# One inference step of a hybrid S5/HGRN2 decoder: HGRN's first level with 32 weight columns, sample values spread by transfers, state-space table products in four partition groups

## Chip, core and metric

The kernel runs on one core of a Trainium2 chip. The core has five engines with a queue each: PE (TensorE), DVE (VectorE), ACT (ScalarE), POOL (GpSimd) and SP (SyncE, which here only issues transfers). They meet through semaphores. The metric is the device time of one execution, in microseconds (us), as the median of several runs.

## What is computed

A two-layer trunk over 512 prompt tokens and 8 sample tokens, 1024 wide, in f32. Each layer adds half an FFN, a mixer, a cross-attention and half an FFN. The mixer is S5 in layer 0 and HGRN2 (8 heads, 128x128 state) in layer 1. Cut to what the change touches:

```python
# S5: 64 groups of 16 channels, each with a 64-dim complex diagonal state
bu = jnp.einsum('btgc,gpc->btgp', ug, b_bar)
a_cum, x_cum = lax.associative_scan(combine, (a_seq, bu), axis=1)
h = x_cum + a_cum * h0[:, None]
y = jnp.einsum('btgp,gcp->btgc', h, c).real + d * ug

# HGRN2 per token (the prompt is done in chunks of 64 tokens; a sample is one step from its given state)
# S_t = diag(f_t) S_{t-1} + k_t v_t^T ,  o_t = S_t^T q_t
att = jnp.einsum('bthk,bshk,btshk->bhts', qc, kc, decay)     # decay: product of f between s and t, causal
s_new = jnp.exp(btot)[..., None] * s + jnp.einsum('bshk,bshv->bhkv', k_dec, vc)
```

## The kernel before

**Linear layers.** All activations lie transposed (channels on partitions, 520 token columns). Weights stream from HBM tile by tile: SP loads `raw` (L965), ACT rounds it to `w_hi` (L1329), DVE makes the rest `w_lo` (L1826), and PE multiplies `w_hi` by both parts of the activations (L3017) and `w_lo` by the upper part (L3022). SP loads slot `j` of a pair again as soon as DVE has made the low part of what lay in it (`lo_ready`). Each engine runs its instructions in the order in which they are written; small work for the mixers is written between the chunks of the linear layers.

**State-space tables (155 to 320 us).** During layer 0's first FFN, POOL builds tables in eight rounds (`table_part`, L736 to L738): `sFe` for the inputs, then `sGe` for the outputs, and counts `s5_tables` after each. PE turns `sFe` (groups F, L2559) and forms the products K of `sGe` with `bZ` (L2565), to which it adds a diagonal `dD` (L2568). A group K has four pairs `u`; for each, two products of 32 rows and 128 columns and one of 16 columns are added up in `bank[0:32, u * 128:...]`. ACT copies the bank to `sKst` (L1466), from which SP writes a block matrix to HBM (L945). Groups 0 to 3 stand in `ffn1_out0`, groups 4 to 7 in `ffn1_in1`.

**HGRN (1540 to 1815 us).** `hg_in` handles one head per turn, spread over three turns: turn `h` projects head `h` (four chunks of weights: forget gate, queries, values, gate), works on head `g = h - 1` and finishes head `e = h - 2`. PE's groups are numbered in one list, `made`, and group `q` uses PSUM bank `q % 4`; it waits until the bank's last group has been emptied. For head `g`: V and K (transposes, L2798), A (attention within chunks by levels: level 32, 16 and 8 pair the later half of a block with its earlier half, L2810; then the rest, L2813), D (increments of the state, L2836), B (L2818: the value vector of each sample, broadcast to all partitions by transposing a column with step 0), O (outputs, L2851 and L2859). For head `e`: S (the samples' outputs, L2784), T, N and R. A level-32 product of a 64-token chunk takes all 64 tokens of `lvl` as weights and the 32 later ones as moving columns; DVE then copies only the wanted part under a mask (`causal`, L2183).

DVE makes the values (`hgV`, L2187), the states (`hS`, L2201 and L2205), then the samples' states `sS` from group B's banks (L2315), then the next low weights. SP stores `hS` and `sS` (L908, L910) and loads the samples' old states (L921).

**The end of HGRN.** When the last head is done, `hg_out` begins: its first two chunks are multiplied head by head (`projected`, L2896), between the last heads' groups.

## Time and profile before

| | |
|---|---|
| median of 3 runs | 2366.99 us (2365.1 to 2368.97) |
| the profiled execution | 2364.88 us |
| its span | 2363.1 us |
| PE, DVE, ACT, POOL busy | 99%, 55%, 37%, 26% |

An instruction's row gives its start, its duration and how many were merged. Matmuls overlap, so what one costs is the distance from its start to the next one's. PE records an f32 product as two matmuls and an f32 transpose as one. The idle time in brackets names what the engine waited for.

### The profile page before, as it was taken

What the parts mean: (1) busy time and instruction counts of PE and PEld (TensorE: products, weight loads), DVE (VectorE), ACT (ScalarE), POOL (GpSimd) and SP (SyncE); (2) the same over time, 40 slices, a digit from 0 to 9 for tenths busy, and PEclk for the clock granted to TensorE, in tenths of its full rate; (3) what the DMA queues carried; (4) which work ended last, traced back from release to release, by engine and by line L of the source; (5) the groups of instructions that cost most, each with busy time, mean ns of one, the idle gap of its engine ahead of it and who ended that gap; (6) DMA issues with size and microseconds to landing.
All of it is one profiled execution on the core that took longest, in us unless ns stands there. A gap on an engine that the chain in (4) does not pass through costs nothing.

```text
span 2363.1 us, 50146 instructions
## 1 busy us (share of the span) xinstructions
PE 2341.2 (99%) x21043; PEld 2280.2 (96%) x21043; DVE 1292.9 (55%) x1906; ACT 871.4 (37%) x1399; POOL 608.2 (26%) x591
## 2 busy tenths in 40 slices
PE   8999999999999999999999999999999999999999
PEld 8999999889979999999999999999999979999999
DVE  6653643864576543445543344577778666443443
ACT  4422333543233231232333233267775233321323
POOL 4779958331103000004121010432222102000003
PEclk9999999999999999999999999999999999999999
DMA  6456445563463333333543333333332653333332
GB/s 169 128 156 151 119 123 156 182 184 107 148 242 101 95 91 91 98 104 87 169 119 106 105 104 116 86 99 103 109 104 81 214 188 90 98 94 94 98 93 95
DMA packets 483707, 289.19 MB, mean 122 GB/s; under 512 B 22289, under 2 KB 466962, under 8 KB 482514
## 3 DMA queue, kind: packets, MB, share of 16 engines
q1 hardware_dynamic: 477856, 280.66, 40.3%
q0 software_dynamic: 560, 1.84, 0.6%
q10 hardware_dynamic: 5122, 4.25, 0.5%
q8 instruction: 129, 2.11, 0.4%
q14 instruction: 40, 0.33, 0.0%
HBM read 258.86 MB, written 27.85 MB: 121 GB/s over the span
## 4 chain that ended last, share of the span: by engine, by line
PE 89%; DVE 4%; POOL 3%; ACT 2%; DMA 1%; issue 1%; SPq 0%; DVEq 0%; POOLq 0%; ACTq 0%
PE lin L3017 50%; PE lin L3022 25%; PE mis L2511 3%; POOL sTmp L737 1%; PE mis L2648 1%; PE mis L2631 1%; POOL sGe L738 1%; PE lin L2598 1%; POOL sGe L736 1%; PE lin L2979 1%; POOL sFe L738 1%; PE lin L2648 0%; DMA raw<-in_xattn_w_kv_dram 0%; PE lin L2760 0%; DVE w_lo L1826 0%
## 5 line engine op out<-in xcount | busy, mean ns | idle before, releaser
L1826 DVE TENSOR_TENSOR w_lo<-raw,w_hi 128x1024 fp32r<-128x1024 f32 (+1 forms) x322 | 463.4, 1439 | 297.7 <-ACT w_hi L1329 297.1
L1329 ACT ACTIVATE w_hi<-raw 128x1024 fp32r<-128x1024 f32 (+1 forms) x328 | 364.9, 1113 | 305.7 <-PE lin L3022 251.3
L3017 PE MATMUL lin<-a_rear,w_hi 128*128 128x264 f32 x3552 | 455.5, 279 | 0.0
L3017 PE MATMUL lin<-a_front,w_hi 128*128 128x256 f32 x3552 | 451.5, 279 | 1.1 <-DVE a_rear L1839 0.7
L3017 PEld LDWEIGHTS lin<-a_rear,w_hi 128*128 128x128 f32 x3552 | 432.6, 188 | 0.0
L3017 PEld LDWEIGHTS lin<-a_front,w_hi 128*128 128x128 f32 x3552 | 424.4, 188 | 4.6 <-issue 1.9
L3022 PE MATMUL lin<-a_rear,w_lo 128*128 128x264 f32 x1776 | 245.2, 278 | 0.0
L3022 PE MATMUL lin<-a_front,w_lo 128*128 128x256 f32 x1776 | 240.5, 277 | 0.9 <-DVE w_lo L1826 0.9
L2390 DVE SCALAR_TENSOR_TENSOR xT<-lin,xT 128x520 f32<-128x520 f32 (+1 forms) x87 | 60.8, 699 | 322.2 <-PE lin L3022 321.5
L1062 POOL TENSOR_TENSOR acc<-xT 128x520 f32<-128x520 f32 x8 | 12.2, 1520 | 864.0 <-DVE xT L2390 835.9
L3022 PEld LDWEIGHTS lin<-a_rear,w_lo 128*128 128x128 f32 x1776 | 223.8, 188 | 0.0
L3022 PEld LDWEIGHTS lin<-a_front,w_lo 128*128 128x128 f32 x1776 | 219.5, 188 | 1.6 <-DVE w_lo L1826 1.5
L1740 ACT ACTIVATE f_front<-t 128x256 fp32r<-128x256 f32 (+1 forms) x88 | 36.9, 419 | 395.1 <-DVE t L2371 395.1
L3017 PE MATMUL lin<-f_rear,w_hi 128*128 128x264 f32 x1386 | 178.1, 281 | 0.0
L3017 PEld LDWEIGHTS lin<-f_rear,w_hi 128*128 128x128 f32 x1386 | 170.5, 188 | 0.1
L3017 PE MATMUL lin<-f_front,w_hi 128*128 128x256 f32 x1386 | 170.3, 276 | 0.0
L3017 PEld LDWEIGHTS lin<-f_front,w_hi 128*128 128x128 f32 x1386 | 163.3, 188 | 0.1
L1736 ACT ACTIVATE t<-t 128x520 f32<-128x520 f32 x88 | 56.5, 642 | 278.6 <-DVE t L2365 278.6
L2369 DVE TENSOR_TENSOR t<-lin,rstd 128x520 f32<-128x520 f32 x88 | 61.5, 699 | 158.5 <-PE lin L3022 158.4
L1066 POOL TENSOR_TENSOR sqt<-xT 128x520 f32 (+1 forms) x54 | 81.9, 1517 | 211.0 <-DVE xT L2390 148.9
L3017 PE MATMUL lin<-g_all,w_hi 128*128 128x264 f32 (+1 forms) x1024 | 128.8, 278 | 0.0
L3017 PEld LDWEIGHTS lin<-g_all,w_hi 128*128 128x128 f32 x1024 | 122.8, 188 | 1.1 <-DVE g_all L1966 1.1
(512 smaller groups left out, 3207.9 us busy)
## 6 DMA issues: line engine op xcount, KB each, us to landing
raw<-in_ffn_w_in_dram SPq DMA_DIRECT2D x176, 512.0 KB, 3.9
raw<-in_ffn_w_out_dram SPq DMA_DIRECT2D x64, 704.0 KB, 4.6
kc<-in_cache_mem_k_dram SPq DMA_DIRECT2D x32, 512.0 KB, 7.0
vc<-in_cache_mem_v_dram SPq DMA_DIRECT2D x16, 1024.0 KB, 9.4
raw<-in_hg_w_in_dram SPq DMA_DIRECT2D x32, 512.0 KB, 4.3
raw<-in_xattn_w_kv_dram SPq DMA_DIRECT2D x16, 512.0 KB, 4.4
raw<-in_s_w_glu_dram SPq DMA_DIRECT2D x16, 512.0 KB, 4.1
raw<-in_xattn_w_q_dram SPq DMA_DIRECT2D x16, 512.0 KB, 3.9
```

The source lines that it names most:

```text
L736: link(eng.tensor_tensor(out[:, e], pv[0], mv[e], ALU.mult))
L738: link(eng.tensor_tensor(out[:, e], out[:, e], tmp, sign))
L1066: step.link(pool.tensor_tensor(sqt[:], tile(xT, m), tile(xT, m), ALU.mult))
L1329: act.activation(w_hi[:, j, 0:kt, :], raw[:, j, 0:kt, :], ACT.Copy).then_inc(hi_ready, 1)
L1736: act.activation(t2[:], t1[:], ACT.Silu).then_inc(gate_out, 1)
L1740: ins = act.activation(tile(out, i), t3[:, cols], ACT.Copy)
L1826: dve.tensor_tensor(low_weights(n, j), raw[:, j, 0:kt, :], w_hi[:, j, 0:kt, :].bitcast(F32), ALU.subtract).then_inc(lo_ready, 1)
L2369: step.link(dve.tensor_tensor(t4[:], lflat(1), rstd[:], ALU.mult))
L2390: dve.scalar_tensor_tensor(out=tile(xT, m), in0=lflat(j), scalar=scale, in1=tile(xT, m), op0=ALU.mult, op1=ALU.add)\
L2511: ins = pe.matmul(kv_bank(c)[:, 0:NM], w[:, e, k, :], x[:, k, :], start=k == 0 and u == 0, stop=k == KD - 1 and u == 2)
L3017: pe.matmul(lpart(j, half), high[:, k, :], (x_lo if u else x_hi)[half][:, k, :], start=start and u == 0 and k == 0, stop=False)
L3022: ins = pe.matmul(lpart(j, half), low[:, k, :], x_hi[half][:, k, :], start=False, stop=k == kt - 1)
```

## The change

1. **Table products.** The four pairs `u` of a group K write to `bank[32 * u:32 * u + 32, 0:128]` rather than to four column ranges of partitions 0 to 31. The eight long products are issued with `u` in the inner loop, and then the four short ones. `sKst` is 128x128 rather than 32x512.
2. **Samples' values.** The groups B are gone. SP stores the eight value columns of a head to a scratch tensor `hg_v` in HBM (`values_out`) and loads that tensor's 4 KB to each of 128 partitions (`vB`, `values_spread`); DVE reads `vB`. The semaphore `sampled` takes the place of B's emptied banks, and `values` on DVE waits until the store before the last has read `hgV`.
3. **Level 32.** The weights are the first 32 tokens of the chunk, and the result goes to 32 partitions of the 64. The other 32 are under the mask.

```diff
@@ -310,6 +310,9 @@
     sRow = at("sRow", [P, 2, P], F32, o_tmp + TILE)
+
+    vB = [at(f"vB{e}", [P, NS, P], F32, (o_hid + 6 * HTILE, o_tmp + 5 * TILE)[e]) for e in range(2)]
+    hg_v = nc.dram_tensor("hg_v", (HH, NS, P), F32, kind="Internal").ap()
     rT = at("rT", [P, NT // 4], F32, o_tmp + 4 * TILE)
@@ -326,7 +329,7 @@
     sGe = [at(f"sGe{e}", [P, 2, 4, CS + 1, SC], F32, o_s0 + 4608 * e) for e in range(2)]
-    sKst = at("sKst", [2 * SC, 4, P], F32, o_s0 + 31360)
+    sKst = at("sKst", [P, P], F32, o_s0 + 31360)
     dD = at("dD", [P, KD, SC], F32, o_s0 + 11520)
@@ -451,7 +454,8 @@
            "scaled_dve", "front", "state_out", "s_decay", "s_out", "squares", "inverse")}
-    rows_in = [sem(f"rows_in{b}") for b in range(NS)]
+    rows_in = [sem(f"rows_in{b}") for b in range(4)]
+    spread_out, spread_in, sampled = sem("spread_out"), sem("spread_in"), sem("sampled")
     consts_done = sem("consts_done")
@@ -624,7 +628,7 @@
         if 0 <= g < HH:
-            made += [("D", (g, 0), "dve"), ("D", (g, 1), "dve"), ("B", (g, 0), "dve"), ("B", (g, 1), "dve")]
+            made += [("D", (g, 0), "dve"), ("D", (g, 1), "dve")]
             made += [("O", (g, 0), "act"), ("O", (g, 1), "act")]
@@ -906,8 +910,23 @@
                 sp.dma_start(o_["hg_p"][0, 0, h], hS[:, NHC - 1, :]).then_inc(hg["state_out"], 16)
-                HG.emptied_of(sp, "B", (h, 1))
+                sp.wait_ge(sampled, h + 1)
                 sp.dma_start(o_["hg_s"][0, :, h].rearrange("b k v -> k b v"), sS[h % 2][:]).then_inc(hg["s_out"], 16)
+
+            def values_out(h):
+
+                sp.wait_ge(used[0], first_pair["hg_in", 1] + 2 * h + 2)
+                sp.dma_start(hg_v[h].rearrange("b v -> v b"), hgV[h % 2][:, SEQ:NT],
+                             allow_slow_non_contiguous=True).then_inc(spread_out, 16)
+
+            def values_spread(h):
+
+                sp.wait_ge(spread_out, 16 * (h + 1))
+                if h >= 2:
+                    sp.wait_ge(sampled, h - 1)
+                    sp.wait_ge(spread_in, 16 * h)
+                src = bass.AP(tensor=hg_v.tensor, offset=h * NS * P, ap=[[0, P], [P, NS], [1, P]])
+                sp.dma_start(vB[h % 2][:], src).then_inc(spread_in, 16)
 
@@ -942,7 +961,8 @@
                                           ap=[[row, SC], [SC * row - SC, CS], [1, P]])
-                            sp.dma_start(dst, sKst[SC * g:SC * (g + 1), u:u + 1, :].to_broadcast([SC, CS, P]))\
+                            r0 = 2 * SC * u + SC * g
+                            sp.dma_start(dst, sKst[r0:r0 + SC, :].unsqueeze(1).to_broadcast([SC, CS, P]))\
                                 .then_inc(s5_k_out, 16)
@@ -968,6 +988,8 @@
                             s5_matrices(i)
+                        if first and j == 0 and ST[n][0] == "hg_out":
+                            values_spread(HH - 1)
                         if first and j == 0 and ST[n][0] == "xo":
@@ -990,8 +1012,13 @@
                             sample_states_in(i // 2)
-                        elif i >= 4:
-                            states(i // 2 - 2)
+                            if i >= 3:
+                                values_spread(i // 2 - 1)
+                        elif i >= 2:
+                            values_out(i // 2 - 1)
+                            if i >= 4:
+                                states(i // 2 - 2)
+                    values_out(HH - 1)
                     return
@@ -1463,7 +1490,7 @@
                         wait(act, s5_k_out, 16 * CS * a)
-                        act.activation(sKst[:], bank[0:2 * SC, :].rearrange("p (j n) -> p j n", j=4), ACT.Copy)\
+                        act.activation(sKst[:], bank[:, 0:P], ACT.Copy)\
                             .then_inc(s5p_void["act"], 1)
@@ -1644,7 +1671,7 @@
                         if h >= 2:
-                            G.emptied_of(act, "B", (h - 2, 1))
+                            act.wait_ge(sampled, h - 1)
                             act.wait_ge(hg["scaled_pool"], POOLS * (h - 1))
@@ -2184,6 +2211,8 @@
                     dve.wait_ge(chunk_done, 2 * p + 3)
+                    if p >= p0 + 4:
+                        dve.wait_ge(spread_out, 16 * ((p - p0) // 2 - 1))
                     dve.tensor_tensor(hgV[b][:], lflat(0), rstd[:], ALU.mult).then_inc(used[0], 1)
@@ -2306,17 +2335,16 @@
                     if 0 <= g < HH:
+                        dve.wait_ge(spread_in, 16 * (g + 1))
                         for f in range(2):
-                            q = G.at("B", (g, f))
                             dve.wait_ge(hg["s_decay"], 2 * g + f + 1)
-                            dve.wait_ge(hg["fill"], q + 1)
                             for u in range(4):
...
                                 ins = dve.scalar_tensor_tensor(
-                                    out=sS[g % 2][:, s_], in0=hg_bank(q)[:, u * P:(u + 1) * P],
+                                    out=sS[g % 2][:, s_], in0=vB[g % 2][:, s_],
                                     scalar=hgK[g % 2][:, SEQ + s_:SEQ + s_ + 1], in1=sS[g % 2][:, s_],
                                     op0=ALU.mult, op1=ALU.add)
-                            ins.then_inc(hg["void_dve"], 1)
+                        ins.then_inc(sampled, 1)
                     if h == HH:
@@ -2560,13 +2588,14 @@
                         pe.wait_ge(s5_tables, 2 * a + 2)
+                        rows = [slice(2 * SC * u, 2 * SC * (u + 1)) for u in range(4)]
+                        for e in range(2):
+                            for u in range(4):
+                                pe.matmul(bank[rows[u], 0:P], bZ[:, e, 4 * a + u, :, :].rearrange("p g c -> p (g c)"),
+                                          sGe[a % 2][:, e, u, 0:CS, :], start=e == 0, stop=False, skip_group_check=True)
                         for u in range(4):
-                            for e in range(2):
-                                pe.matmul(bank[0:2 * SC, u * P:(u + 1) * P],
-                                          bZ[:, e, 4 * a + u, :, :].rearrange("p g c -> p (g c)"),
-                                          sGe[a % 2][:, e, u, 0:CS, :], start=e == 0, stop=False)
-                            ins = pe.matmul(bank[0:2 * SC, u * P:u * P + SC], ident[:, 2 * SC * u:2 * SC * (u + 1)],
-                                            dD[:, a, :], start=False, stop=True)
+                            ins = pe.matmul(bank[rows[u], 0:SC], ident[:, rows[u]], dD[:, a, :], start=False, stop=True,
+                                            skip_group_check=True)
                     ins.then_inc(s5p_fill, 1)
@@ -2778,7 +2807,7 @@
                 if what == "S":
-                    G.emptied_of(pe, "B", (a, 1))
+                    pe.wait_ge(sampled, a + 1)
                     for b in range(NS):
@@ -2807,15 +2836,12 @@
                             late = lvl[u][:, c].rearrange("p (b a t) -> p b a t", a=2, t=level)[:, :, 1, :]
-                            ins = pe.matmul(bank[rows, t * HC // 2:(t + 1) * HC // 2].rearrange("p (b t) -> p b t", t=level),
-                                            lvl[u][:, c], late, start=True, stop=True)
+                            early = level if 2 * level == HC else HC
+                            ins = pe.matmul(bank[rows.start:rows.start + early, t * HC // 2:(t + 1) * HC // 2]
+                                            .rearrange("p (b t) -> p b t", t=level),
+                                            lvl[u][:, c.start:c.start + early], late, start=True, stop=True)
                         else:
                             ins = pe.matmul(bank[rows, t * HC:(t + 1) * HC], dgK[:, c], dgQ[:, c], start=True, stop=True)
-                elif what == "B":
-                    h, f = a
-                    for u in range(4):
-                        b = SEQ + 4 * f + u
-                        ins = pe.transpose(bank[:, u * P:(u + 1) * P], hgV[h % 2][:, b:b + 1].to_broadcast([P, P]), ident[:])
                 else:
@@ -2934,8 +2960,6 @@
                         hg_increments(g)
-                        hg_group("B", (g, 0))
-                        hg_group("B", (g, 1))
                     if h == HH:
```

PE at a group K. Before (the transposes of `sTF`, then the group, then the next chunk):

```order
L2559 MATMUL mis<-ident,sTF_235 128x128 x3
L2565 MATMUL mis<-sGe_199,bZ 32x128 [waits s5_tables,s5p_void_dve]
L2565 MATMUL mis<-sGe_199,bZ 32x128
L2568 MATMUL mis<-dD,ident 32x16
L2565 MATMUL mis<-sGe_199,bZ 32x128 x2
L2568 MATMUL mis<-dD,ident 32x16
L2565 MATMUL mis<-sGe_199,bZ 32x128 x2
L2568 MATMUL mis<-dD,ident 32x16
L2565 MATMUL mis<-sGe_199,bZ 32x128 x2
L2568 MATMUL mis<-dD,ident 32x16
L3017 MATMUL lin<-f_rear_61,w_hi 128x264 [waits used0,hi_ready]
```

And after:

```order
L2587 MATMUL mis<-ident,sTF_237 128x128 x3
L2594 MATMUL mis<-sGe_201,bZ 32x128 [waits s5_tables,s5p_void_dve]
L2594 MATMUL mis<-sGe_201,bZ 32x128 x7
L2597 MATMUL mis<-dD,ident 32x16 x4
L3041 MATMUL lin<-f_rear_61,w_hi 128x264 [waits used0,hi_ready]
```

The products and the waits are the same; the short ones have moved behind the long ones.

SP at the end of HGRN, from the last loads of `hg_w_in` to the stores of the last head. Before:

```order
L965 DMA raw<-in_hg_w_in_dram 128x8x128 [waits lo_ready] x2
L921 DMA sS_177<-in_state_hgrn_dram 128x8x128 [waits hg_fill,hg_s_out]
L965 DMA raw<-in_hg_w_out_dram 128x8x128 [waits lo_ready] x2
L908 DMA out_hg_p_dram<-hS 128x128 [waits hg_void_dve]
L910 DMA out_hg_s_dram<-sS_176 128x8x128 [waits hg_void_dve]
L908 DMA out_hg_p_dram<-hS 128x128 [waits hg_void_dve]
L910 DMA out_hg_s_dram<-sS_177 128x8x128 [waits hg_void_dve]
```

And after (`hg_v<-hgV` is `values_out`, `vB<-hg_v` is `values_spread`; the three in the middle belong to the heads 6, 7 and 7):

```order
L985 DMA raw<-in_hg_w_in_dram 128x8x128 [waits lo_ready] x2
L940 DMA sS_177<-in_state_hgrn_dram 128x8x128 [waits hg_fill,hg_s_out]
L929 DMA vB_187<-hg_v 128x1024 [waits spread_in,sampled,spread_out]
L919 DMA hg_v<-hgV_163 128x8x1 [waits used0]
L985 DMA raw<-in_hg_w_out_dram 128x8x128 [waits lo_ready]
L929 DMA vB_188<-hg_v 128x1024 [waits spread_in,sampled,spread_out]
L985 DMA raw<-in_hg_w_out_dram 128x8x128 [waits lo_ready]
L912 DMA out_hg_p_dram<-hS 128x128 [waits hg_void_dve]
L914 DMA out_hg_s_dram<-sS_176 128x8x128 [waits sampled]
L912 DMA out_hg_p_dram<-hS 128x128 [waits hg_void_dve]
L914 DMA out_hg_s_dram<-sS_177 128x8x128 [waits sampled]
```

The first load of `hg_w_out` now stands behind the store of head 7's values, which waits for `used0`, and the second behind the load of `vB`, which waits for that store.

## Rows read from the trace of the kernel before

**Rows 1.** The page: engine busy time (us, share, instructions), and the chain's shares.

```profile
PE 2341.2 (99%) x21043; PEld 2280.2 (96%) x21043; DVE 1292.9 (55%) x1906; ACT 871.4 (37%) x1399; POOL 608.2 (26%) x591
...
PE 89%; DVE 4%; POOL 3%; ACT 2%; DMA 1%; issue 1%; SPq 0%; DVEq 0%; POOLq 0%; ACTq 0%
```

**Rows 2.** Timeline of PE, first group K: start, us, engine, line, operation, out<-in, count.

```profile
157.70 0.62 PE L2565 MATMUL mis<-sGe,bZ 128*32 128x128 f32 x4
158.16 0.21 PE L2568 MATMUL mis<-dD,ident 128*32 128x16 f32 x2
158.22 0.60 PE L2565 MATMUL mis<-sGe,bZ 128*32 128x128 f32 x4
...
159.80 2.39 PE L3017 MATMUL lin<-f_rear,w_hi 128*128 128x264 f32 x18
```

**Rows 3.** Timeline of PE: the first rows of groups K 1 to 4.

```profile
176.13 0.62 PE L2565 MATMUL mis<-sGe,bZ 128*32 128x128 f32 x4
...
194.56 0.62 PE L2565 MATMUL mis<-sGe,bZ 128*32 128x128 f32 x4
...
213.60 0.60 PE L2565 MATMUL mis<-sGe,bZ 128*32 128x128 f32 x4 [0.54 <-POOLq L1190]
...
239.11 0.62 PE L2565 MATMUL mis<-sGe,bZ 128*32 128x128 f32 x4
```

**Rows 4.** Timeline of POOL: the last operation of tables 1 to 4.

```profile
172.98 1.43 POOL L738 TENSOR_TENSOR sGe<-sGe,sTmp 128x576 f32<-128x576 f32 x1
...
192.80 1.43 POOL L738 TENSOR_TENSOR sGe<-sGe,sTmp 128x576 f32<-128x576 f32 x1
...
212.00 1.41 POOL L738 TENSOR_TENSOR sGe<-sGe,sTmp 128x576 f32<-128x576 f32 x1
...
231.34 2.29 POOL L738 TENSOR_TENSOR sGe<-sGe,sTmp 128x576 f32<-128x576 f32 x1
```

**Rows 5.** Timeline of PE, one turn of HGRN.

```profile
1603.21 0.64 PE L2784 MATMUL mis<-sS,hgQ 128*32 128x128 f32 x16
1603.79 0.66 PE L2798 MATMUL mis<-ident,hgV 128*128 128x128 f32 x4
1604.28 0.60 PE L2798 MATMUL mis<-ident,outK 128*128 128x128 f32 x4
1604.81 1.59 PE L2810 MATMUL mis<-lvl 128*64 128x32 f32 x48
1606.33 0.44 PE L2790 MATMUL mis<-ident,sRow 128*128 128x128 f32 x2
...
1620.18 1.09 PE L2818 MATMUL mis<-ident,hgV 128*128 128x128 f32 x8
1621.02 2.13 PE L3017 MATMUL lin<-a_front,w_hi 128*128 128x256 f32 x16
```

**Rows 6.** Timelines of SP, DVE, ACT and PE at the end of HGRN.

```profile
1764.22 0.37 SPq L921 DMA_DIRECT2D sS<-in_state_hgrn_dram  x1
1770.22 0.37 SPq L965 DMA_DIRECT2D raw<-in_hg_w_out_dram  x1
...
1782.11 0.69 DVE L2187 TENSOR_TENSOR hgV<-lin,rstd 128x520 f32<-128x520 f32 x1
...
1787.72 1.22 DVE L1826 TENSOR_TENSOR w_lo<-raw,w_hi 128x1024 fp32r<-128x1024 f32 x1
...
1784.99 1.05 ACT L1329 ACTIVATE w_hi<-raw 128x1024 fp32r<-128x1024 f32 x1
...
1791.86 1.06 ACT L1329 ACTIVATE w_hi<-raw 128x1024 fp32r<-128x1024 f32 x1
...
1789.77 0.39 PE L2896 MATMUL lin<-h_hi,w_hi 128*128 128x256 f32 x1
```

**Rows 7.** Transfers: line, queue, operation, count, KB each, median us to landing.

```profile
raw<-in_hg_w_out_dram SPq DMA_DIRECT2D x8, 512.0 KB, 3.8
...
s_t<-zeros POOLq DMA_DIRECT2D x1, 64.0 KB, 2.8
```

## The prediction, made before the change was timed

> **What bounds the kernel now.** I read the page first. PE is busy for 99% of the span and holds 89% of the chain that ended last [rows 1]. So work pays when it comes off PE in a place where nothing else is late, and a delay elsewhere costs what it makes PE wait. Then I read the two stages that the change touches, engine by engine: the state-space tables (155 to 320 us) and HGRN (1540 to 1815 us). The execution that these rows come from took 2364.88 us (span 2363.1, 1.8 outside it). The median of the runs is 2366.99. I sum a difference and take it from the median.
>
> **The table products (group K, eight times).** Before, 12 products of one group all go to output partitions 0 to 31. The first starts at 157.70 and the next chunk's product at 159.80, so a group holds PE for 2.10 us [rows 2]. An f32 product is recorded as two matmuls. Four records with 128 columns take 0.46 us (115 ns each), two with 16 columns 0.06 us (30 ns each) [rows 2]. After, the same 16 + 8 records go to four partition groups in turn. The nearest row is the HGRN samples' product L2784: also 32 weight columns, 128 moving columns and four partition groups in turn. Its 16 records start at 1603.21 and the next work at 1603.79: 0.58 us, 36 ns each [rows 5]. With the dD products at their present 30 ns: 0.58 + 8 x 0.03 = 0.82 us, 1.28 less than now. Bounds: nothing gained if the turns don't overlap, and 2.10 - 24 x 0.03 = 1.38 if even the long ones come at 30 ns.
>
> Does it pay eight times? Each group waits for a table that POOL writes. POOL's last operations for tables 1, 2 and 3 end at 172.98 + 1.43 = 174.41, 194.23 and 213.41 [rows 4]. PE starts those groups at 176.13, 194.56 and, after waiting 0.54 us for POOL, 213.60 [rows 3]. With 1.28 less for group 0, PE comes to group 1 at 174.85, just behind the table. With 2.56 less it would come to group 2 at 192.0 and wait over 2 us. It would come to group 3 early again and start at 213.60 as before. So what groups 0, 1 and 2 save is handed back as a wait for POOL, and from group 3 on PE is ahead by group 3's own 1.28. For group 4 the table ends at 233.63 and PE starts at 239.11 [rows 3, 4]: 5.5 us of room, and from group 3 to group 4 PE takes 25.5 us and POOL 20.2, so the room grows. Sum: 5 x 1.28 = 6.4 us, of 10.2 that eight would give; bounds 0 and 6.9.
>
> ACT empties a bank of 128x128 in place of 32x512: shorter and not on the path. The 64 transfers of sKst only read other partitions.
>
> **The samples' values (groups B, eight heads).** Removed: eight broadcasts by transpose per head, from 1620.18 to the next chunk's 1621.02, 0.84 us [rows 5], 6.7 us in eight heads. In their place come per head a store of 1024 single words (SP), a load of 512 KB to 128 partitions, and DVE's eight operations read SBUF instead of PSUM, which I price equal. For the normal heads both transfers are hidden. The store waits for the values on DVE, and in SP's order the next weight load waits for a split that DVE makes later still. The load follows `sS` (1764.22 for head 7) [rows 6]. So head 6's load comes over 15 us before its samples are computed, which is between the values at 1782.11 and the split at 1787.72. With B gone the banks of R wait for the states rather than the samples, which is looser.
>
> The end of HGRN is another matter. There the store of head 7's values stands in SP's row ahead of the first load of `hg_w_out`. Before, that load went out at 1770.22 [rows 6], over 14 us ahead of its use: ACT rounds it at 1784.99, DVE makes its low part at 1787.72 (1.22 us), and PE takes it at 1789.77. After, it can't go before the values are there, at 1782.11 + 0.69 = 1782.80. With 0.4 for the store's issue, 3.8 us to landing [rows 7] and 0.5 for sharing: 1787.5. Then ACT 1.05 and DVE 1.22 give 1789.8, where PE without group B of this head would be ready at 1788.93. PE waits about 0.9 us. If the load must wait for the whole store, the nearest row is the zeros' store of 64 KB, 1024 pieces of 64 B: 2.8 us [rows 7]. Then 1782.85 + 2.8 + 3.8 + 1.05 + 1.22 = 1791.7, and PE waits 2.8 us. The second load waits for the store to land and for head 7's 512 KB load to be issued: 1782.85 + 2.8 + 0.5 + 3.8 + some 1.3 for sharing = 1791.3. ACT takes it at 1791.86 now [rows 6] and would come about 1 us later itself, so it is just hidden; each us later than that costs one.
>
> From there to 1813 PE, DVE and ACT hand small pieces to each other. DVE goes through without a pause, so that what PE saves in groups B of heads 6 and 7 helps it little: I count 0.5 of 1.7 us. Sum for HGRN: 6 x 0.84 = 5.0, + 0.5, less 1.5 (between 0.9 and 2.8) = 4.0 us gained. Bounds: 6.7, and by the nearest rows 5.0 - 2.8 = 2.2; rival 3 is what slower transfers would make of it.
>
> The Trainium skill (DMA: Bandwidth & Descriptors, the rules for kernel authors and the specifications) says that a strided last dimension becomes one descriptor per element and that pieces under 512 B are read, modified and written. It gives no price for 4 B. By this rule the store is the worst kind of transfer, and it is what speaks for rival 3. Rows 7's 64 B pieces fall under the same rule and took 2.8 us, so the trace doesn't bear out a high price.
>
> **The first level (32 weight columns for 64).** All 48 level records take 1606.33 - 1604.81 = 1.52 us, 31.7 ns each [rows 5], and records with 32 weight columns and 16 moving ones 30 ns [rows 2]. So 16 x 8 x 1.7 ns = 0.2 us are gained. Between the first level and the second the width of the weights now changes once more. From the transposes of outK (four in 0.53 us) to the levels it changes as well, against 0.49 us for the four of hgV with no change behind them [rows 5]: 0.04 us each, 0.3 in eight heads. I take 0. Bounds: 0.3 lost, and 2.0 gained if the spacing halves with the weights.
>
> The Trainium skill (TensorEngine Tiling (Array Packing), key properties) says that a change of tiling mode drains TensorE, and that this is what each further width change costs. It gives no time for it; rival 5 is what it would make of the sum, and the 0.04 us above speak against it.
>
> **Sum.** 6.4 + 4.0 + 0 = 10.4 us: 2366.99 - 10.4 = 2356.6 us.
>
> **Rivals.**
> 1. The end of HGRN costs more. For: 128 rows all read the same 4 KB, and no row of before does that; the second load of `hg_w_out` stands behind it, and ACT and DVE wait for that before all else in their next turn. Against: it is as many bytes as any weight load. With 5 us more: 5.4 us gained, 2361.6.
> 2. The products in four partition groups don't overlap, because two of them add to the same words. Then only HGRN gains: 2366.99 - 4.0 = 2363.0. Against: L2784's 36 ns, in the same kind of order.
> 3. Slower: the store of single words holds the queue. At 0.25 us a word, 64 words for each of 16 engines take 16 us. The first load of `hg_w_out` then lands at 1802.7 and PE waits until 1805, 16 us, against 6.4 + 5.5 gained: 4.1 lost, 2371. It decides from a store of 12 us on; at 6 us it takes HGRN's gain and no more. Against: 2.8 us for 1024 pieces in rows 7.
> 4. DVE is not in PE's way at the end, the wait for the first load falls short, and the first level gains its bound: 6.9 + 6.7 + 2.0 = 15.6, 2351.4.
> 5. Each further change of width lets the matmul before it run out. One record of 16 columns is 0.21 - 0.03 = 0.18 us long [rows 2], so 8 x 0.18 = 1.4 us are lost: 9.0 gained, 2358.0. Against: 0.04 us at such a change in rows 5.
>
> **Numbers.** The forecast has 0.66, rival 1 0.14, rival 2 0.07, rival 3 0.04, rival 4 0.05, rival 5 0.04. 0.2% is 4.7 us, about what can be told from no change. The forecast and rivals 4 and 5 are beyond it. Rival 1 lies near it, so half counts on each side, and rival 2 is within it: faster 0.66 + 0.05 + 0.04 + 0.07 = 0.82, same 0.07 + 0.07 = 0.14, slower 0.04. Range 2352 to 2363.5: the low end takes in nearly all the upper bounds, the high end rival 1 and rival 2.
>
> **What would show it.** Right: a K group of 0.8 us; PE waiting some 2 us for POOL before group 2 and again before group 3; group 4 at 237.8; the B rows gone, and the heads 0.84 us closer together; the first `hg_w_out` load issued behind the store, and PE waiting 1 to 3 us for its low part. Wrong: a K group of 2 us (rival 2); no wait for POOL (then all eight pay, and it is 3.8 us faster); a store that lands after more than 6 us; PE waiting in every head for `w_lo` or, through DVE, for vB.

## The result and the profile after

| | before | changed |
|---|---|---|
| median (14 runs each) | 2367.16 us | 2372.87 us |
| lowest and highest | 2364.47, 2372.54 | 2371.14, 2377.0 |
| the profiled execution, its span | 2364.88, 2363.1 | 2375.26, 2373.5 |

The ratio is 1.0027, with a 95% interval of 1.002 to 1.0035: about 6 us slower, where 10.4 us faster was forecast. The profiled executions lie 2.3 us under and 2.4 us over their medians, so between the two traces there are 10.4 us rather than 5.7.

The page after, engine busy time and the chain's shares, beside [rows 1]:

```profile
PE 2333.4 (98%) x20979; PEld 2270.0 (96%) x20979; DVE 1305.0 (55%) x1906; ACT 869.9 (37%) x1399; POOL 607.3 (26%) x591
...
PE 84%; DVE 6%; POOL 3%; ACT 3%; DMA 2%; issue 2%; SPq 0%; DVEq 0%; ACTq 0%; POOLq 0%
```

PE is busy for 7.8 us less and the span is 10.4 us longer, so PE now waits, and the chain runs over DVE and DMA more often. DVE is busy for 12.1 us more, though the change gave it no further operation.

**The tables** went as forecast. PE's timeline of the first group K, and the first rows of groups 1 to 4, beside [rows 2, 3]:

```profile
157.71 0.64 PE L2594 MATMUL mis<-sGe,bZ 128*32 128x128 f32 x16
158.17 0.23 PE L2597 MATMUL mis<-dD,ident 128*32 128x16 f32 x8
158.33 2.87 PE L3041 MATMUL lin<-f_rear,w_hi 128*128 128x264 f32 x22
...
174.66 0.64 PE L2594 MATMUL mis<-sGe,bZ 128*32 128x128 f32 x16
...
194.56 0.75 PE L2594 MATMUL mis<-sGe,bZ 128*32 128x128 f32 x16 [2.84 <-POOLq L1217]
...
213.53 0.65 PE L2594 MATMUL mis<-sGe,bZ 128*32 128x128 f32 x16 [0.40 <-POOLq L1217]
...
237.44 0.65 PE L2594 MATMUL mis<-sGe,bZ 128*32 128x128 f32 x16
```

A group takes 0.62 us in place of 2.10. Group 2 waits 2.84 us for POOL and starts at 194.56, to the hundredth where it did before; from group 3 on every group counts. At the first work of S5 PE is 7.6 us ahead (404.39 for 411.98).

**HGRN** gave it back. From the timelines of PE I took four marks: V0, head 0's first transposes of `hgV`; S0, S5 and S6, the samples' outputs of heads 0, 5 and 6. For before they are 1571.08, 1603.21, 1763.47 and 1791.75; after, 1566.21, 1605.36, 1761.40 and 1801.21. The stretches in us, for the change and the kernels timed beside it (ident_read, lo_first, act_store and price_list are told of in their sections):

| kernel | V0 to S0 | S0 to S5 | S5 to S6 | S6 to end |
|---|---|---|---|---|
| before | 32.1 | 160.3 | 28.3 | 571.4 |
| changed | 39.2 | 156.0 | 39.8 | 572.3 |
| k_only | 32.2 | 160.3 | 28.3 | 571.3 |
| k_level | 32.2 | 159.4 | 28.3 | 571.3 |
| values_only | 35.8 | 156.8 | 39.0 | 571.8 |
| load_first | 36.8 | 156.0 | 30.0 | 571.1 |
| rows32 | 35.5 | 158.8 | 30.8 | 572.1 |
| pairs8 | 35.3 | 156.1 | 32.0 | 573.3 |
| head0_first | 31.9 | 159.5 | 29.9 | 571.2 |
| five_heads | 32.2 | 158.5 | 28.6 | 575.1 |

So the change gains 4.2 us in the five middle turns and loses 7.0 before them and 11.5 behind them.

The end of HGRN after, timelines of SP, ACT, DVE and PE, beside [rows 6]:

```profile
1781.12 0.37 SPq L919 DMA_DIRECT2D hg_v<-hgV  x1
1781.54 0.57 SPq L985 DMA_DIRECT2D raw<-in_hg_w_out_dram  x1
1791.15 0.33 SPq L929 DMA_DIRECT2D vB<-hg_v  x1
...
1795.94 1.06 ACT L1356 ACTIVATE w_hi<-raw 128x1024 fp32r<-128x1024 f32 x1 [12.55 <-DMA raw<-in_hg_w_out_dram]
...
1797.03 1.23 DVE L1853 TENSOR_TENSOR w_lo<-raw,w_hi 128x1024 fp32r<-128x1024 f32 x1 [9.61 <-ACT w_hi L1356]
...
1798.31 0.58 PE L2922 MATMUL lin<-h_hi,w_hi 128*128 128x256 f32 x1 [11.19 <-DVE w_lo L1853]
```

The store goes out at 1781.12. The load of `vB` waits for it and nothing else by then, and goes out at 1791.15: it took 10.0 us until the 4 KB counted as landed. The weight load issued 0.4 us behind the store is there at 1795.94, 14.4 us after its issue, where 3.8 is the median [rows 7]. PE waits 11.19 us. Of the DMA, the trace shows these packets from 1782 to 1783 and from 1783 to 1786:

```profile
DMA packets 1059, 0.01 MB, mean 14 GB/s; under 512 B 1040, under 2 KB 1059, under 8 KB 1059
...
DMA packets 20, 0.01 MB, mean 3 GB/s; under 512 B 0, under 2 KB 20, under 8 KB 20
```

So the words' own packets are through within about 1 us. What takes the time stands behind them: for 3 us hardly anything moves, then the transfers creep along at 32 GB/s until 1793 and go on at 262 GB/s.

The same stands at head 0, in SP's, ACT's, DVE's and PE's timelines, and with it a second cause:

```profile
1559.16 0.37 SPq L919 DMA_DIRECT2D hg_v<-hgV  x1
1562.31 6.30 SPq L985 DMA_DIRECT2D raw<-in_hg_w_in_dram  x2
...
1574.67 1.06 ACT L1356 ACTIVATE w_hi<-raw 128x1024 fp32r<-128x1024 f32 x1 [6.65 <-DMA raw<-in_hg_w_in_dram]
...
1576.26 0.66 PE L2840 MATMUL mis<-lvl 128*64 128x32 f32 x16 [1.85 <-ACT vTok L1663]
...
1592.76 4.62 DVE L2343 SCALAR_TENSOR_TENSOR sS<-vB,hgK,sS 128x128 f32<-128x128 f32 x8
1597.30 1.22 DVE L1853 TENSOR_TENSOR w_lo<-raw,w_hi 128x1024 fp32r<-128x1024 f32 x1
...
1598.57 2.08 PE L3046 MATMUL lin<-a_front,w_lo 128*128 128x256 f32 x8 [2.94 <-DVE w_lo L1853]
```

The load behind the store is 12.4 us under way; ACT waits for it, makes `vTok` late, and PE waits 1.85 us. Later DVE's eight sample operations take 4.62 us (2.15 before), the low part behind them is late, and PE waits 2.94 us for it.

**The clock.** Windows of PE after: busy time (instructions), granted clock, DMA share, GB/s.

```profile
190.00:194.00 4.00, 1.72 (x16) 1.00 0.99 276
194.00:198.00 4.00, 3.44 (x36) 0.62 0.90 188
...
412.00:420.00 8.00, 7.55 (x50) 0.59 0.34 87
...
1597.00:1606.00 9.00, 7.43 (x49) 0.62 1.08 83
...
1788.00:1798.00 10.00, 0.00 (x0) 0.55 0.68 144
1798.00:1803.00 5.00, 4.69 (x33) 0.53 0.42 125
1803.00:1810.00 7.00, 6.60 (x113) 1.00 0.02 4
```

Before, the granted clock is 1.00 in these stages. In this trace it falls to the lower level (1.2 GHz) behind each of PE's waits of 2.8 to 11 us and stays there for the first microseconds of work. It also falls behind the 1.85 us at 1574 (0.74 from 1575 to 1580). So such a wait costs more than its length: at 1798 to 1803 another 5 x 0.47 = 2.3 us. It isn't so every time: values_only has a wait of 3.05 us in head 0 too, and its clock there is 1.00. At S5 the same two short waits (0.88 and 0.45 us) stand in both traces, and the clock falls behind them only in the one of after; PE's lead shrinks there from 7.6 to 5.2 us.

### The profile page after: what moved, and what is told of

The parts are those of the page before. It is cut to its first block, busy times and chain, and to the rows that moved or that the text cites. A ratio compares the mean times of both kernels' runs of the same rounds, so it can differ in the third digit from the quotient of the medians.

```text
span 2373.5 us, 50038 instructions
## 1 busy us (share of the span) xinstructions
PE 2333.4 (98%) x20979; PEld 2270.0 (96%) x20979; DVE 1305.0 (55%) x1906; ACT 869.9 (37%) x1399; POOL 607.3 (26%) x591
## 4 chain that ended last, share of the span: by engine, by line
PE 84%; DVE 6%; POOL 3%; ACT 3%; DMA 2%; issue 2%; SPq 0%; DVEq 0%; ACTq 0%; POOLq 0%
PE lin L3041 47%; PE lin L3046 24%; PE mis L2539 4%; POOL sTmp L741 1%; DVE sS L2343 1%; DVE w_lo L1853 1%; PE mis L2677 1%; PE mis L2660 1%; POOL sGe L742 1%; DMA raw<-in_hg_w_out_dram 1%; PE lin L2789 1%; DVE hS L2234 1%; PE lin L2784 1%; PE lin L3003 1%; DMA raw<-in_hg_w_in_dram 1%
```

## Experiments

price_list and act_store were run once each. The others were timed in four groups, each beside the kernel before, whose medians there were 2368.1, 2367.6, 2367.5 and 2367.7 us.

### k_only and k_level: the parts that don't touch the queue

k_only is the kernel before with the diff of the table products. k_level adds

```diff
-    bank[rows, ...], lvl[u][:, c], late, start=True, stop=True)
+    bank[rows.start:rows.start + early, ...], lvl[u][:, c.start:c.start + early], late, start=True, stop=True)
```

> The kernel before with the table products in four partition groups and nothing else. The traces of before and of the change have the eight groups 7.6 us shorter in sum at the start of S5 (411.98 against 404.39), after POOL's cap on groups 0 to 2. Theory 1 (this part pays and the transfers eat it): 2367.2 - 7.6 = 2359.6, or about 2362 if the clock drop of 2.4 us at S5 (414 to 420 us, granted 0.50) comes back with the earlier start. Rival (the table part itself costs later, by clock drops after POOL's wait of 2.8 us): within 0.1% of before, 2365 to 2369.

> As the kernel with the table products alone, plus the first level's 32 weight columns; groups B stay. In the trace of the change a head's 48 level records start 1.43 us before the next work, against 1.52 before: 8 x 0.09 = 0.7 us less than the table part alone. Theory 1: 0.7 us faster than that kernel. Rival (the extra change of width between levels drains PE): up to 0.3 us slower than it. Either is near what can be told; the spacing of the rows decides.

Measured: k_only 2359.61, ratio 0.9963 (0.995 to 0.9976); k_level 2360.39, ratio 0.9969 (0.9957 to 0.9981). Both are faster than before, by some 8 us; theory 1 holds for the tables. The medians don't tell the two apart. The traces do, a little: from S0 to S5 a head is 32.05 us in k_only and 31.88 in k_level, 0.17 less, and the level records take 1.43 us for 1.52. There is no sign of a cost at the changes of width.

### values_only: the third part alone

The kernel before with the diff of the samples' values and nothing else.

> The values by transfers as in the changed kernel, with the table products and the first level of before. If the parts add up: the changed kernel less the gain of the other two parts, 2372.9 + 7.2 = 2380. If the clock's state makes them depend on each other (the table part brought a fall of the clock in S5 that costs 2.4 us in one profile): 2377 to 2380.

Measured: 2378.2, ratio 1.0051 (1.0037 to 1.0065): 10.7 us slower. The parts add up within the intervals: 7.7 us gained by k_level and 10.7 lost here make 3.0 lost, and 5.7 lost together were measured (as ratios 0.9969 x 1.0051 = 1.0020 against 1.0027, with 0.0012 to 0.0014 of doubt in each factor). The time lies in the second range, 2377 to 2380, but that doesn't show that the clock is what ties the parts together. The stretches are those of the changed kernel but for V0 to S0, which is 3.4 us shorter, at a granted clock of 1.00.

### load_first: the order of the queue

```diff
-                    values_out(HH - 1)            # behind the last turn of hg_in
-                        if first and j == 0 and ST[n][0] == "hg_out":
-                            values_spread(HH - 1)
                         if first and j == 1 and ST[n][0] == "hg_out":
+                            values_out(HH - 1)
+                            values_spread(HH - 1)
```

> The changed kernel with the store and the spreading load of head 7 behind both first loads of hg_out, still 1024 single words. Theory 1: the loads go out at about 1768 and 1778 as before, PE's wait of 11.2 us and the clock drop behind it go, the cost at head 0 stays: 2372.9 - 11.2 - 2.8 = 2359. Rival 1 (the store slows any transfer beside it, also those in flight): PE still waits several us in the last head, above 2363. Rival 2 (head 7's samples now wait for vB): DVE waits for vB after 1797 and the same microseconds come back.

Measured: 2362.25, ratio 0.9978 (0.997 to 0.9987). PE's wait of 11.2 us is 1.5 us, and S5 to S6 is 30.0 us in place of 39.8. That is 3.2 us over the 2359 of theory 1; the medians are 10.6 us under the changed kernel, the traces 13.4 from V0 on. The cost at head 0 stays, and DVE's part of it is seen alone. PE's timeline of load_first:

```profile
1572.02 0.66 PE L2839 MATMUL mis<-lvl 128*64 128x32 f32 x16 [0.68 <-ACT vTok L1662]
...
1594.33 1.19 PE L3045 MATMUL lin<-a_front,w_lo 128*128 128x256 f32 x8 [3.00 <-DVE w_lo L1852]
```

Here head 7's store stands behind both loads, whose packets are through by 1777. SP's timeline, and the DMA packets from 1776 to 1778 and from 1778 to 1781:

```profile
1775.69 0.37 SPq L919 DMA_DIRECT2D hg_v<-hgV  x1
1785.88 0.34 SPq L929 DMA_DIRECT2D vB<-hg_v  x1
...
DMA packets 1221, 0.09 MB, mean 45 GB/s; under 512 B 1054, under 2 KB 1221, under 8 KB 1221
...
DMA packets 0, 0.00 MB, mean 0 GB/s; under 512 B 0, under 2 KB 0, under 8 KB 0
```

From 1782 to 1786 there is no packet either, and between them one of an instruction load. The store still counts as landed only 10.2 us after its issue, with nothing beside it. So the 10 us are the words' own, and they are not time in which packets move. What goes on in them no trace here shows.

### rows32, pairs8, price_list: what a store of single words costs

rows32 and pairs8 keep the order of the changed kernel. rows32 stores a partition's eight words as one piece of 32 B, pairs8 as four of 8 B; DVE reads `vB` with the step that follows.

```diff
-    sp.dma_start(hg_v[h].rearrange("b v -> v b"), hgV[h % 2][:, SEQ:NT], ...)
+    sp.dma_start(hg_v[h], hgV[h % 2][:, SEQ:NT])                                         # rows32, hg_v is (HH, P, NS)
+    sp.dma_start(hg_v[h].rearrange("a v c -> v a c"), hgV[...].rearrange("v (a c) -> v a c", c=2), ...)   # pairs8
```

> The changed kernel with the samples' values stored as 128 pieces of 32 B (scratch laid out value by sample) in place of 1024 single words; same order of issues, same 4 KB to each partition. Theory 1 (single words make the store slow and hold the load behind it): the store lands in 2 to 3 us in place of 10, PE's wait at the end of HGRN falls from 11.2 to 1 to 3 us, the waits of head 0 (1.9 and 2.9 us) go, and the clock drops behind them (about 2.8 and 5 us) too: 2352 to 2357. Rival (the order of the queue or the broadcast load costs, whatever the pieces): 2371 to 2374 as the changed kernel.

> The kernel with groups B kept (2360.4 us); SP stores value columns in another number and size of pieces in each head, waits until they have landed, and then issues one piece of 64 B, whose start shows the landing. Heads 0 to 7: 1024, 512, 256 and 128 pieces of 4 B, 512 of 8 B, 256 of 16 B, 128 of 32 B, 2048 of 4 B. Theory 1 (a price per piece): about 10 us for 1024, 5.5 for 512, 1.5 for 128 of 32 B as well as of 4 B, 5.5 for 512 of 8 B, 3 for 256 of 16 B, 19 for 2048. Rival (a price for words under some size): 512 of 8 B and 256 of 16 B far cheaper than as many pieces of 4 B. Its own time is of no interest.

Measured for rows32: 2366.54, ratio 0.9998 (0.9989 to 1.0006), between both theories. SP's timeline at the end:

```profile
1782.04 0.34 SPq L919 DMA_DIRECT2D hg_v<-hgV  x1
1782.43 0.43 SPq L984 DMA_DIRECT2D raw<-in_hg_w_out_dram  x1
1783.46 0.32 SPq L928 DMA_DIRECT2D vB<-hg_v  x1
```

Theory 1 is right for the store: 1.4 us to landing for 10.0, and PE's wait there is 2.0 us for 11.2. The wait for `vTok` in head 0 is gone too. What it left out is DVE: the wait for `w_lo` in head 0 stays, at 3.5 us. The step of 32 B makes the median sample operation 438 ns rather than 341, and from head 1 on PE waits 0.4 us in each head for DVE's `hO` (S0 to S5 is 158.8 us, not 156.0).

SP's timeline of price_list, for heads 0, 3, 4 and 7 (the store, then the piece of 64 B that waited for it):

```profile
1559.20 0.37 SPq L926 DMA_DIRECT2D hg_v<-hgV  x1
1569.59 0.26 SPq L928 DMA_DIRECT2D hg_w<-hgV  x1
...
1655.01 0.34 SPq L926 DMA_DIRECT2D hg_v<-hgV  x1
1662.70 0.25 SPq L928 DMA_DIRECT2D hg_w<-hgV  x1
...
1686.79 0.37 SPq L926 DMA_DIRECT2D hg_v<-hgV  x1
1690.68 0.25 SPq L928 DMA_DIRECT2D hg_w<-hgV  x1
...
1782.39 0.37 SPq L926 DMA_DIRECT2D hg_v<-hgV  x1
1793.24 0.25 SPq L928 DMA_DIRECT2D hg_w<-hgV  x1
```

| pieces | 2048 x 4 B | 1024 x 4 B | 512 x 4 B | 256 x 4 B | 128 x 4 B | 512 x 8 B | 256 x 16 B | 128 x 32 B |
|---|---|---|---|---|---|---|---|---|
| us | 10.9 | 10.4 | 8.0 | 8.6 | 7.7 | 3.9 | 2.8 | 3.1 |

A price per piece is refuted: 128 words take 7.7 us and 2048 take 10.9. The size decides: 512 pieces of 8 B land in half the time of 512 of 4 B, and 128 of 32 B in 3.1 us (1.4 in rows32) against 7.7 for 128 of 4 B. These are one sample each, with weight loads partly beside them, so a microsecond either way is open.

> The changed kernel, same order in SP's row, with the values stored as 512 pieces of 8 B (two samples side by side) in place of 1024 of 4 B, and vB read by DVE with a step of 8 B (with 128 pieces of 32 B the step of 32 B had cost 0.1 us an operation, 438 against 341 ns). From the price list: the store lands in 3.9 us in place of 10.4. So the load of hg_out behind it lands about 6.5 us earlier, PE waits some 4 to 5 us in place of 11.2 and head 0's load is 6.5 us earlier too, which its slack covers; head 0's wait for w_lo behind DVE's sample operations (3.0 us) stays. If the step of 8 B is free: 2372.9 - 6.5 - 2 to 3 of low clock = 2363.5; if it costs like that of 32 B (the heads 32.0 us apart and not 31.4): 2366.5. Rival (the words' size isn't the cause): 2371 to 2374.

Measured: 2364.45, ratio 0.9985 (0.9976 to 0.9994), 1 us from the first number. The load of `vB`, which waits for the store, went out 3.6 us behind it, PE waited 3.4 us, and the heads were 31.2 us apart (156.1 / 5) at an operation's median of 342 ns, so a step of 8 B is free.

### act_store: the queue or the engines?

```diff
+    act.wait_ge(used[0], p + 2)          # head 7, in ACT's row; SP only waits for used0 ahead of the first load of hg_out
+    act.dma_start(hg_v[h].rearrange("b v -> v b"), hgV[h % 2][:, SEQ:NT], ...)
```

> The kernel with groups B kept (2360.4 us); head 7's 1024 single words are stored from ACT's queue at about 1776 to 1782, and SP issues the first load of hg_w_out only once the values are there, as in the changed kernel, but with no store ahead of it in its own queue. Nothing reads the words. Rival A (the 16 engines are busy with the words, whichever queue they come from): the load lands 10 us or more after its issue, PE waits about 10 us. Rival B (a queue takes its transfers in turn and only that queue is held): it lands about 4 us after its issue and PE waits 1 to 3 us.

SP's and ACT's timelines:

```profile
1780.26 0.99 SPq L968 DMA_DIRECT2D raw<-in_hg_w_out_dram  x2
```

```profile
1780.27 0.46 ACTq L1707 DMA_DIRECT2D hg_v<-hgV  x1
...
1791.09 1.06 ACT L1334 ACTIVATE w_hi<-raw 128x1024 fp32r<-128x1024 f32 x1 [7.86 <-DMA raw<-in_hg_w_out_dram]
```

The load was 10.8 us under way with the store in another queue, and PE waited 6.3 us. Rival A's landing came true and rival B's didn't: transfers of either queue are slowed. PE's wait lies between the two. Rival A's reason, engines busy with the words, isn't what the packets show: 1032 of the 1040 in ACT's queue are through by 1785, and from 1785 to 1787 the DMA moved 31 GB/s. Two loads of 512 KB went out together here, and the stores of `hS` and `sS` (64 and 512 KB) at 1783.2 and 1785.3, so not all of the 10.8 need be the words'.

### ident_read, lo_first, head0_first: DVE's operations

ident_read is k_level with another source for the vector:

```diff
-    out=sS[g % 2][:, s_], in0=hg_bank(q)[:, u * P:(u + 1) * P],
+    out=sS[g % 2][:, s_], in0=ident[:],
```

> The kernel with the table products and the first level changed and groups B kept (2360.4 us), in which DVE's sample operations take the 128x128 identity in SBUF as the vector instead of group B's bank (so the samples' states and outputs are not computed); no transfer is added. Theory M2 (an operation with both arrays in SBUF is held by POOL's operations beside it): eight operations of a head take 3.5 to 4.6 us as in the changed kernel, single ones over 1 us, and PE waits about 2.5 us for w_lo in head 0: 2363 to 2366. Rival (vB is slow for its transfers, or its place in SBUF): 2.15 us a head, 2360.

Measured: 2365.09, ratio 0.9987 (0.9978 to 0.9996), 4 to 5 us slower than k_level. DVE's groups of these operations in HGRN (busy us, mean ns), first k_level, then ident_read:

```profile
L2316 DVE SCALAR_TENSOR_TENSOR sS<-mis,hgK,sS 128x128 f32<-128x128 f32 x64 | 17.1, 341 | 0.0
```

```profile
L2316 DVE SCALAR_TENSOR_TENSOR sS<-ident,hgK,sS 128x128 f32<-128x128 f32 x64 | 28.2, 508 | 0.0
```

The changed kernel has the same 28.2 us and 508 ns with `vB`. So neither the transfers nor the place of `vB` makes them long; theory M2 holds. What POOL does beside them is in the timelines of DVE and POOL, ident_read, with PE's wait behind them:

```profile
1592.02 4.60 DVE L2316 SCALAR_TENSOR_TENSOR sS<-ident,hgK,sS 128x128 f32<-128x128 f32 x8
1592.54 1.31 POOL L1296 TENSOR_TENSOR outK<-outK,hgK 128x512 f32<-128x512 f32 x1
1593.82 1.34 POOL L1298 TENSOR_TENSOR inQ<-inQ,hgQ 128x512 f32<-128x512 f32 x1
...
1597.81 1.18 PE L3026 MATMUL lin<-a_front,w_lo 128*128 128x256 f32 x8 [2.10 <-DVE w_lo L1827]
```

DVE's timeline of k_level at the same place:

```profile
1588.55 2.15 DVE L2316 SCALAR_TENSOR_TENSOR sS<-mis,hgK,sS 128x128 f32<-128x128 f32 x8
```

k_level has the same two operations of POOL (1589.07 and 1590.30) beside eight of DVE from the bank, and they take 2.15 us. The longest single operation in ident_read is 1382 ns, in k_level 347. It is about as long as one of POOL's. The wait of 2.10 us fits that of the changed kernel (2.94), where PE comes 0.84 us earlier for want of groups B. From V0 to S6 ident_read takes 4.3 us more than k_level, which is nearly the difference of the medians (4.7).

The Trainium skill (SBUF — State Buffer, "SBUF: two separate sides") says that VectorE and GpSimd share one pair of SBUF ports, that an operation of VectorE with two SBUF inputs needs it against a GpSimd operation that reads SBUF, and that it is held for the whole instruction. These rows agree: 1382 ns beside POOL, 347 with one input in PSUM.

lo_first and head0_first are load_first with the next low part ahead of the samples' states in DVE's row, in every head and in head 0 alone:

```diff
+                    if 0 < h < HH:                  # head0_first: if h == 1
+                        split(p + 2, 0, hg_chunk(h, 2))
                     if 0 <= g < HH:
                         dve.wait_ge(spread_in, 16 * (g + 1))
```

> The kernel with both first loads of hg_out ahead of head 7's store (2362.3 us), and in DVE's row the next low part of the weights ahead of the samples' states in every head. Theory M2 (DVE's sample operations are longer when they read vB in SBUF: 4.6 us in the first head and 3.5 to 4.1 in the others, where the bank took 2.15; PE waits behind them for w_lo, 3.0 us at 1594 and the clock falls): that wait goes and with it some 3 us of low clock: 2362.3 - 3 - 2.5 = 2357, and the small waits of later heads stay. Rival (the loads of head 0 held by the store carry that wait): no change, 2361 to 2363.

> The kernel with both first loads of hg_out ahead of head 7's store (2362.3 us), with DVE's next low part ahead of the samples' states in head 0 alone. Theory M2: PE's wait of 3.0 us for w_lo in head 0 falls below 0.5 us and the low clock behind it goes; the later heads keep 31.3 us, which the move cost them in the kernel that made it everywhere (31.95): 2362.3 - 3.3 = 2359. Rival (the single words' hold on the loads of head 0 takes that place): 2361 to 2363.

Measured: lo_first 2366.29, ratio 0.9995 (0.9986 to 1.0004), 4 us slower than load_first, of which the traces show only 0.7 from V0 to the end (the rest is open); head0_first 2361.51, ratio 0.9974 (0.9964 to 0.9984). In both the wait of 3.0 us is gone (0.15 and 0.2 us are left), so it was DVE's order. The times are not those of theory M2: 9 us over it, and for head0_first in the rival's range. In lo_first the sample operations fall behind POOL's and are short again (355 ns in the mean, from the same `vB`). But what follows them in DVE's row is late; PE's timeline of head 1 there:

```profile
1636.26 0.66 PE L2826 MATMUL mis<-ident,outK 128*128 128x128 f32 x4 [1.59 <-DVE hO L2253]
```

Such a wait of 0.45 us then comes in every head, and ACT's `hO` costs PE up to 2.9 us in one turn. In head0_first V0 to S0 is back at 31.9 us, but the next turn takes 33.7, and by S5 most of it is given back: 191.4 us from V0 to S5 against load_first's 192.8. DVE has to win its lead once, in one turn or in the other.

### five_heads: a version meant to beat all

```diff
+    MOVED = [1, 2, 3, 4, 5]            # the others keep groups B and read the bank
```

> Table products and first level as changed; values by transfers for heads 1 to 5 only, groups B for heads 0, 6 and 7. Theory (the transfers pay where DVE and the queue have room, and cost at both ends): the heads 31.3 us apart as in the kernel with the loads first, against 31.9 with groups B: 5 x 0.6 = 3.0 us under the kernel with groups B everywhere: 2360.4 - 3.0 = 2357.4, the best so far. Rival (the longer sample operations make DVE late at another place once the starts differ): 2359 to 2362, no better than groups B everywhere.

Measured: 2360.24, ratio 0.9966 (0.9955 to 0.9978). It beats before and the changed kernel and is no better than k_level or k_only; the rival holds. Its 40 operations with `vB` take 516 ns in the mean and its 24 from the bank 337. Head 1's turn takes 32.75 us, since DVE comes late once (0.77 us for `w_lo`, 0.41 for `hO`), and V0 to S6 is 219.4 us against 219.9 in k_level. (Its 575.1 us to the end hold a wait of 2.1 us for a load of `vc` and a granted clock of 0.91 from 1920 to 1940, which are not of this part.)

## Why the prediction was wrong

**Tables: right.** Forecast: a group K of 0.82 us, waits at groups 2 and 3, group 4 at 237.8, 6.4 us in all. Measured: 0.62 us, waits of 2.84 and 0.40, group 4 at 237.44, 7.6 us at the start of S5 (five groups and more of 1.48 each), and 8.5 us between the medians of k_only and its own before. The 16 long records came 29 ns apart (0.46 us), under the bound's 30; I had taken 36 from the samples' product. The order of the products and their place in the bank changed together with the partition groups, so which of these gives the 29 ns no run here tells. Not forecast was that the wait of 2.84 us takes the clock down behind it (0.62 from 194 to 198). That uses up 4 x 0.38 = 1.5 us of what group 2 saves, and is why the wait before group 3 is 0.40 us and not some 2.

**First level: right in kind.** Forecast 0 within 0.3 lost and 2.0 gained; the trace shows 0.17 us a head, 1.4 in eight, too little for the medians.

**Values: the wrong step.** The forecast was 4.0 us gained; k_level against the changed kernel shows 12.5 lost, and values_only 10.7. It failed in these terms:

- *The store's landing*, "the nearest row is the zeros' store of 64 KB, 1024 pieces of 64 B: 2.8 us", and PE waiting 0.9 to 2.8 us. It took 10.0 us, and PE waited 11.2. The count of pieces was right, and the nearest row stood on the wrong side of a step in size: pieces of 8, 16 and 32 B land in 1.4 to 3.9 us, words of 4 B in 8 to 11.
- *The load behind it.* I let it share for 0.5 us. It took 14.4 us, and act_store shows that another queue would not have freed it.
- *DVE reads SBUF instead of PSUM, "which I price equal".* It is 508 ns for 341 in the mean, because of POOL beside it. That is 11.1 us of DVE's time, 3.0 us of PE's in head 0 (2.1 if PE comes there no earlier, as in ident_read), and part of what the other heads should have gained: with the first level's 0.17 taken off, 31.88 - 31.21 = 0.67 us a head in place of 0.84.
- *Head 0.* The sum had the end of HGRN and "the normal heads", and no line for the first turn, where DVE has no lead over PE yet (before, PE already waits 0.45 us for `w_lo` there and in no later head). It cost 7.0 us: the two causes above and the clock.
- *The clock.* No term had it. By the rows it is some 2.3 us at the end, in head 0 the 3.4 us that values_only doesn't have at full clock, and 2.4 us at S5.

Rival 3 named the right cause, place and side (2371, with a chance of 0.04). Its mechanism was not right: no run shows a price of 0.25 us a word (16 us for 1024), the words take 10 us whether there are 1024 or 2048, and it isn't the queue alone that is held. Its threshold was 12 us, and 10 were enough, since head 0 pays as well. That its 2371 comes so near 2372.87 is luck: it had 16 us for 11.2 at the end, and nothing for head 0's 7.0. What I held against it, the row of 64 B pieces, was the weak point.

The rule that I cited there from the Trainium skill (DMA: Bandwidth & Descriptors, "Rules for kernel authors" and "Specifications") spoke for the rival, and for the 4 B words these runs bear it out. Its line at 512 B they don't: 64 B pieces took 2.8 us, and pieces of 8 to 32 B 1.4 to 3.9.

PE's lead over before in the two traces, in one line: 7.6 us at S5's start, 5.2 behind it, 4.9 at V0; then -7.0, +4.2, -11.5 and -0.9 us, which is 10.4 behind, the difference of the spans.

Open: what happens between the words' last packet and their landing, and why other transfers are slow meanwhile; why the clock falls behind the same waits in one execution and not in another. Single profiles also differ by up to 5 us before the change does anything. PE's start of S5 lies between 404.4 and 409.5 us in kernels with the same table part, and that difference is there at 50 us already (the same product starts at 50.33 in the changed kernel and 55.43 in k_only), behind the first loads of the prompt. The traces of before and after start alike (50.46 and 50.33), so their ledger is right in its places, and in its sizes as far as the clock allows; the medians carry the verdicts.

## What to carry to other kernels

A transfer taken off an engine is not free because it is small: ask for the size of its contiguous piece, and when only larger pieces are in the trace, keep the chance of a step, not a slope. Go by when its semaphore comes, not by when its packets are through. Ask what stands behind it in the queue and beside it on the DMA engines, at the first and the last turn of a loop too, where nothing has a lead. When an operand moves from PSUM to SBUF, look at what POOL does in the same microseconds; and when a saving is under 1 us a turn, check that the engine which takes over the work is not the one that the next turn waits for.

## What the runs showed of the hardware

- A store of 4 B words to HBM lands after 7.7 to 10.9 us for 128 to 2048 words; 8, 16 and 32 B pieces after 1.4 to 3.9 us. The packets of 1024 words are through in about 1 us, and with no packet beside them they still landed after 10.2 us (load_first). Loads of 512 KB behind or beside the 1024 words took 10.8 to 14.4 us (medians of 3.8 and 4.3 before), from another queue too.
- DVE's `scalar_tensor_tensor` of 128x128 f32 takes 341 ns from PSUM with POOL busy beside it, and up to 1382 ns with both arrays in SBUF (mean 508).
- A step of 8 B in one SBUF operand is free (342 ns); one of 32 B costs 0.1 us (438 ns).
- f32 products of 32 weight and 128 moving columns, sent to four partition groups in turn, come 29 ns a record, against 115 when pairs of them go to one group (their order and place in the bank differ too).
- Behind a wait of PE of 2.8 us and more the granted clock was mostly, not always (3.05 us in values_only), at its lower level for the next 3 to 6 us of work. It fell behind shorter ones too: 1.85 us in head 0, and 0.88 and 0.45 us at S5 in one trace and not in the other.
